# A two-block model in fp32 on one core: first block reordered, gates by tanh, linear-attention levels in 32-column tiles

## The reference, cut to what matters

```python
h = x
for i in range(DEPTH):                       # 2
    proj = rmsnorm(h, norm_g[i]) @ w_in[i]
    # hq, hf, hi: linear attention, 4 heads of 128;  hgo, hz: its gates
    # nq, kcm, vcm, ksl, vsl, kwn, vwn, ngate: sparse attention, 8 query heads of 64, 2 key heads;  nz: its gate
    log_f = log(lb + (1 - lb) * sigmoid(hf)); k = (1 - lb) * sigmoid(-hf)
    # S_t = diag(f_t) S_{t-1} + k_t v_t^T,  o_t = S_t^T q_t
    o_hg  = rmsnorm(hgrn2_chunkwise(hq, log_f, k, hi), hgrn_onorm_g[i])
    y_hg  = o_hg * sigmoid(hgo) * silu(hz)
    # o_cmp over 15 compressed blocks, o_slc and o_win over the tokens (causal)
    y_nsa = (g0 * o_cmp + g1 * o_slc + g2 * o_win) * silu(nz)
    h = h + concat([y_hg, y_nsa]) @ w_out[i]
    h = h + sigmoid(rmsnorm(h, ple_norm_g[i]) @ w_pg[i]) * (p[i] @ w_pp[i])
```

## Time and profile before

| | us |
|---|---|
| median of 3 runs | 1172.01 (1171.93 to 1172.96) |
| the profiled execution | 1172.76 |
| its span, first to last instruction | 1170.9 |
| TensorE busy | 1080.4 |
| vector engine busy | 704.9 |
| scalar engine busy | 580.2 |

### The profile page before, as it was taken

How to read it: one execution, slowest core, us unless ns; L and a number is a source line. 1 busy time by engine, 2 the same in 40 slices (tenths; PEclk the granted TensorE clock), 3 DMA queues, 4 the chain that set the end, 5 groups by cost and what they waited for, 6 DMA issues and landing times.

```text
span 1170.9 us, 20111 instructions
## 1 busy us (share of the span) xinstructions
PE 1080.4 (92%) x8425; PEld 1021.6 (87%) x8425; DVE 704.9 (60%) x1011; ACT 580.2 (50%) x818; POOL 4.9 (0%) x13
## 2 busy tenths in 40 slices
PE   3999888798998887998999999999899899999997
PEld 3998776798997776998998999999888689999996
DVE  5566555656566555567675766666544547676674
ACT  4533455555524446365744555454544536455543
POOL 1000000000000000000000000000000000000000
PEclk8999899899999999899999999999898899999998
DMA  8542522244544321263463655556244335555530
GB/s 284 170 120 71 189 72 73 72 129 147 175 115 137 99 84 61 73 211 104 133 209 126 198 182 180 185 184 193 74 149 140 108 108 165 189 185 181 179 108 36
DMA packets 144741, 163.91 MB, mean 140 GB/s; under 512 B 6072, under 2 KB 135424, under 8 KB 144672
## 3 DMA queue, kind: packets, MB, share of 16 engines
q1 hardware_dynamic: 143752, 161.46, 43.0%
q10 hardware_dynamic: 632, 1.30, 0.3%
q0 software_dynamic: 288, 0.14, 0.0%
HBM read 161.85 MB, written 1.05 MB: 139 GB/s over the span
## 4 chain that ended last, share of the span: by engine, by line
PE 74%; DVE 10%; ACT 9%; issue 3%; DMA 2%; SPq 1%; ACTq 0%; DVEq 0%
PE ps L423 22%; PE ps L424 21%; PE ps L425 21%; ACT panels_high L1093 3%; DVE panels_low L1562 3%; ACT probs L1079 2%; PE ps L626 2%; PE ps L503 2%; PE ps L439 1%; DMA panels<-in_w_in 1%; DVE neg_max L1585 1%; DVE probs L1601 1%; PE ps L509 1%; PE ps L986 1%; DVE gate_o L2038 1%
## 5 line engine op out<-in xcount | busy, mean ns | idle before, releaser
L423 PE MATMUL ps<-input_high,panels_low 128*128 128x256 f32 x1792 | 523.0, 292 | 31.1 <-DVE input_low L1542 14.2
L424 PE MATMUL ps<-input_low,panels_high 128*128 128x256 f32 x1792 | 514.8, 287 | 0.0
L425 PE MATMUL ps<-input_high,panels_high 128*128 128x256 f32 x1792 | 514.7, 287 | 0.0
L1562 DVE TENSOR_TENSOR panels_low<-panels,panels_high 128x2048 fp32r<-128x2048 f32 (+1 forms) x146 | 330.3, 2265 | 277.9 <-ACT panels_high L1093 271.2
L423 PEld LDWEIGHTS ps<-input_high,panels_low 128*128 128x128 f32 x1792 | 351.8, 196 | 38.8 <-issue 26.4
L424 PEld LDWEIGHTS ps<-input_low,panels_high 128*128 128x128 f32 x1792 | 351.8, 196 | 0.8 <-issue 0.5
L425 PEld LDWEIGHTS ps<-input_high,panels_high 128*128 128x128 f32 x1792 | 351.5, 196 | 0.0
L1093 ACT CAST panels_high<-panels 128x2048 fp32r<-128x2048 f32 (+1 forms) x146 | 274.6, 1882 | 148.4 <-PE ps L425 128.3
L423 PE MATMUL ps<-ffn_hidden_high,panels_low 128*128 128x256 f32 x352 | 100.7, 286 | 3.8 <-DVE ffn_hidden_low L2052 3.8
L424 PE MATMUL ps<-ffn_hidden_low,panels_high 128*128 128x256 f32 x352 | 101.0, 287 | 0.0
L425 PE MATMUL ps<-ffn_hidden_high,panels_high 128*128 128x256 f32 x352 | 100.8, 286 | 0.0
(11 more groups left out here) (271 smaller groups left out, 1120.3 us busy)
## 6 DMA issues: line engine op xcount, KB each, us to landing
panels<-in_ffn_up SPq DMA_DIRECT2D x44, 1024.0 KB, 5.1
panels<-in_w_in SPq DMA_DIRECT2D x32, 1024.0 KB, 5.5
panels<-in_ffn_down SPq DMA_DIRECT2D x22, 1024.0 KB, 4.9
panels<-in_mix_w_in SPq DMA_DIRECT2D x20, 1024.0 KB, 5.4
panels<-in_w_out SPq DMA_DIRECT2D x8, 1024.0 KB, 5.1
panels<-in_w_pg SPq DMA_DIRECT2D x8, 1024.0 KB, 5.2
panels<-in_mix_w_out SPq DMA_DIRECT2D x8, 1024.0 KB, 6.3
panels<-in_w_pp SPq DMA_DIRECT2D x2, 1024.0 KB, 5.0
```

Of the source, the lines that this page charges most:

```text
L423: pe.matmul(dst, w[1], x[0], start=start, stop=False if not kw else True, **kw)
L424: pe.matmul(dst, w[0], x[1], start=False, stop=False if not kw else True, **kw)
L425: return pe.matmul(dst, w[0], x[0], start=False, stop=stop, **kw)
L1562: V.tensor_tensor(low_slots[slot][:, 0:size], raw[n % SLOTS][:, 0:size], high_slots[slot][:, 0:size].bitcast(F32), ALU.subtract).then_inc( ...
```

## The change

It does six things in the first block.

- Levels by blocks of 32 tokens. Levels 0 to 5 are computed for the four diagonal 32x32 blocks alone, each in its own 32-column tile of the array, and copied under a narrower mask (32 columns a head in place of 128) into a new buffer `decay_blocks` (`AB`). Level 6 computes two 32x32 blocks, level 7 one of 64x64, and both are copied without a mask straight to `AD`. ACT spreads the blocks of `AB` into `AD` (`spread`, four copies).
- Order on TensorE. Gate chunks stand after `hid4`, after the rotated queries, after the last level, after `cross`, after the outputs, after unit 0, and in rounds 0 to 5. `hid` comes ahead of the rotation; `kc` and `vc` ahead of the last level, `kcss` right after the third chunk, `oss` after the scores of compressed keys. `hgo0` uses bank 6, `kc` and `kcss` bank 5.
- Gates by tanh. ACT copies `hz` and `nz` as they are and takes tanh(x/2) from the same bank; one more tanh covers `hgo`. DVE then uses sigmoid(x) = (1 + tanh(x/2))/2, with the factors put in the last product.
- The mixing is spread over the rounds: `mix` halves in rounds 2 and 3, `nsa_gate` halves in rounds 4 and 5, the first two quarters split after round 5.
- The first two output panels are cut by rows (`output_rows`): their first four row blocks are multiplied in round 6 and after round 7, the rest after the last unit. Banks 2 to 5.
- Norm sums of the residual use bank 0, and `pp` banks 7, 6, 1 and 2.

```diff
@@ levels on TensorE
                     for j in range(4):
                         s = (2 * g + j // 2) * T + (j % 2) * P
-                        ins = pe.matmul(ps[b][:, j * P:(j + 1) * P], KQ[:, s:s + P], QP[:, s:s + P],
-                                        start=True, stop=True)
+                        if n < NBLK_LVL:
+                            where = [(BLK * c, BLK, j * BLK, s + BLK * c, s + BLK * c) for c in range(NBLK)]
+                        elif n == NBLK_LVL:
+                            where = [(64 * e, BLK, j * BLK, s + 64 * e, s + 64 * e + BLK) for e in range(2)]
+                        else:
+                            where = [(0, 64, j * 64, s, s + 64)]
+                        for row, w, col, k, q in where:
+                            ins = pe.matmul(ps[b][row:row + w, col:col + w], KQ[:, k:k + w], QP[:, q:q + w],
+                                            start=True, stop=True, tile_position=(0, row), skip_group_check=True)
@@ gate chunks
-                    b = 1 if key[0] == "hgo0" else 0
+                    b = 6 if key[0] == "hgo0" else 0
@@ after hid4
                 todo(("hidden_parts",))
+                gate_chunk()
                 some(1)
+                (hid, as below)
                 (rotated queries)
                 some(1)
-                drained(pe, f"hid4_{l}")
-                begin(f"hid_{l}", 3)
-                ...
-                todo(("hidden",))
+                gate_chunk()
                 (rotated keys)
                 todo(("k_pad",))
-                gate_chunk()
+                pe.wait_ge(w2_landed, 48 * (l + 1))
+                pe.wait_ge(hidden_ready, l + 1)
+                product(f"kc_{l}", 5, 32, W2[:, 0:P], HID[:, 0:32])
+                product(f"vc_{l}", 3, 64, HIDV[:, :], W2[:, P:P + 64])
+                todo(("cmp_kv",))
                 some(16)
                 gate_chunk()
+                pe.wait_ge(kcsq_ready, l + 1)
+                product(f"kcss_{l}", 5, 32, head_ones, KC[:, 32:64])
+                todo(("kc_norm",))
                 (cross)
+                todo(("spread",))
                 todo(("cross",))
+                gate_chunk()
                 ...
+                pe.wait_ge(spread_ready, l + 1)
                 (outputs)
                 todo(("o_square",))
                 gate_chunk()
                 (scores of compressed keys)
-                gate_chunk()
+                pe.wait_ge(osq_ready, l + 1)
+                for g in range(2):
+                    product(f"oss{g}_{l}", 5 + g, 512, ones, SQ[:, g * 512:(g + 1) * 512])
+                todo(("o_norm",))
                 unit(0)
+                gate_chunk()
                 (transposes of the compressed probabilities)
-                gate_chunk()
@@ the rounds
+                def output_rows(g, ks):
+                    key, b = (f"wo{g}", l), out_banks[g]
+                    if ks[0] == 0:
+                        begin(f"wo_{l}_{g}", b)
+                        split(key)
+                    for j in range(2):
+                        for k in ks:
+                            pe.wait_ge(y_ready, 4 * l + k // 2 + 1)
+                            ins = product3(...)
+                    if ks[-1] == ND - 1:
+                        done(f"wo_{l}_{g}", ins)
+                        release(key)
                 for u in range(8):
                     todo(("normalise", u))
                     if u < 7:
                         unit(u + 1)
-                    else:
-                        todo(("mix",))
                     gate_chunk()
+                    if u == 0:
+                        todo(("gate_tanh",))
+                    if u in (2, 3):
+                        todo(("mix", u - 2))
+                    if u in (4, 5):
+                        todo(("nsa_gate", u - 4))
+                    if u == 6:
+                        output_rows(0, range(0, 4))
                     if u > 0:
                         weigh(u - 1)
                     turn(f"n{l}", u, pidx + u)
                     todo(("turned", u))
-                    if u == 6:
-                        todo(("sigmoids",))
+                    if u == 5:
+                        todo(("mixed",))
+                output_rows(1, range(0, 4))
                 weigh(7)
                 todo(("on",))
+                for ks in (range(4, 6), range(6, 8)):
+                    for g in range(2):
+                        output_rows(g, ks)
-                output(f"wo_{l}_", l, 2)
+                norm_sum(nidx, 0, (0,))
+                for g in (2, 3):
+                    two_chunks(f"wo_{l}_{g}", out_banks[g], (f"wo{g}", l))
+                    norm_sum(nidx, 0, (g - 1,))
@@ ACT
+                    if step == "copy" and arg[0] in tanh_dest:
+                        name = f"{arg[0]}_{l}"
+                        full(act, name)
+                        nc.scalar.copy(dest[arg[0]], bank(name)[:, :])
+                        f(tanh_dest[arg[0]], bank(name)[:, :], ACT.Tanh, scale=0.5).then_inc(free(name), 1)
+                    elif step == "spread":
+                        act.wait_ge(level_ready, 16 * l + 2 * NBLK_LVL)
+                        for c in range(NBLK):
+                            r = slice(BLK * c, BLK * (c + 1))
+                            ins = nc.scalar.copy(v3(AD, 8)[r, :, r], v3(AB, 8)[r])
+                        ins.then_inc(spread_ready, 1)
+                    elif step == "gate_tanh":
+                        f(SG[:, :], SG[:, :], ACT.Tanh, scale=0.5).then_inc(sig_ready, 1)
@@ DVE
                     elif kind == "mix":
+                        s = slice(arg[0] * 512, (arg[0] + 1) * 512)
+                        link(V.scalar_tensor_tensor(HZ[:, s], FG[:, s], 1.0, HZ[:, s], ALU.add, ALU.mult))
+                        link(V.scalar_tensor_tensor(HZ[:, s], SG[:, s], 1.0, HZ[:, s], ALU.add, ALU.mult))
+                        V.scalar_tensor_tensor(Y[:, s], QP[:, s], 0.25, HZ[:, s], ALU.mult,
+                                               ALU.mult).then_inc(yf_ready, 1)
+                    elif kind == "nsa_gate":
+                        link(V.scalar_tensor_tensor(NZ[:, s], VH[:, s], 1.0, NZ[:, s], ALU.add, ALU.mult))
+                    elif kind == "mixed":
+                        mixed_low(l, 0)
+                        mixed_low(l, 1)
                     elif kind == "on":
+                        full(dve, f"on1_{l}")
+                        V.scalar_tensor_tensor(Y[:, 1536:2048], bank(name)[:, :], 0.5, NZ[:, 512:1024],
+                                               ALU.mult, ALU.mult).then_inc(free(name), 1)
+                        mixed_low(l, 2)
                         mixed_low(l, 3)
```

More of the change, by code:

```diff
@@ L28 @@
 NLVL = 8
+BLK = 32
+NBLK = P // BLK
+NBLK_LVL = 6
 ALU = mybir.AluOpType
@@ L725, in _ @@
                 todo(("hidden_parts",))
+                gate_chunk()
                 some(1)
+                drained(pe, f"hid4_{l}")
+                begin(f"hid_{l}", 3)
+                for kv in range(2):
+                    ins = pe.matmul(ps[3][:, kv * 32:(kv + 1) * 32], HP[:, kv * P:(kv + 1) * P],
+                                    const("sum_of_four"), start=True, stop=True)
+                done(f"hid_{l}", ins)
+                todo(("hidden",))
                 pe.wait_ge(rope_ready, l + 1)
@@ L736, in _ @@
                 some(1)
-                drained(pe, f"hid4_{l}")
-                begin(f"hid_{l}", 3)
-                for kv in range(2):
-                    ins = pe.matmul(ps[3][:, kv * 32:(kv + 1) * 32], HP[:, kv * P:(kv + 1) * P],
-                                    const("sum_of_four"), start=True, stop=True)
-                done(f"hid_{l}", ins)
-                todo(("hidden",))
+                gate_chunk()
                 pe.wait_ge(k_rope_ready, l + 1)
@@ L781, in _ @@
                 todo(("o_square",))
-                pe.wait_ge(kcsq_ready, l + 1)
-                product(f"kcss_{l}", 0, 32, head_ones, KC[:, 32:64])
-                todo(("kc_norm",))
                 gate_chunk()
-                pe.wait_ge(osq_ready, l + 1)
-                for g in range(2):
-                    product(f"oss{g}_{l}", 5 + g, 512, ones, SQ[:, g * 512:(g + 1) * 512])
-                todo(("o_norm",))
                 pe.wait_ge(kc_ready, l + 1)
```

100 lines of the change are left out of this document (52 added, 48 removed).

## The result

| | before | after |
|---|---|---|
| median, us | 1171.97 (1170.58 to 1172.96, 4 runs) | 1158.22 (1155.53 to 1159.57, 4 runs) |
| ratio | | 0.9888, interval 0.9867 to 0.9909 |
| the profiled execution | 1172.76 | 1159.57 |
| its span | 1170.9 | 1157.7 |

The account below looks back on a forecast made before the run. TensorE's work (92% busy), its waits and its clock were taken to bound the kernel. Levels -5.2, walk -5.0 and clock +1.7 gave -8.5 us from the 1172.01 median: 1163.5 us, range 1152 to 1175.

Parts of the forecast that it names:

- The levels on TensorE: Narrow column tiles: 0.2 us less for each of 13 levels a layer, 5.2 less in all (10.4 less to 5.2 more).
- narrow tiles cheap, waits milder: Rival: levels 0.4 us less each, 5.2 more gained, two bank-0 waits shrink by 3 us; 1155 us, chance 0.23.
- my sum: Levels -5.2, walk -5.0, one more half-clock phase +1.7: -8.5 us, thus 1163.5 us; chance 0.46.
- The vector engine's copies: Narrower masked level copies on DVE: 6 us a layer saved, only 0.3 to 0.4 on a chain, contained in the walk.
- The walk: Reordered work from the hidden products on: waits 19.8 and clock 5.3 where 27 were, 2.5 us less a layer.
- compressed keys, for the hidden values: After two gate chunks, TensorE waits 1.9 us for DVE's low parts, level and hidden activation.
- chunk 3, bank 0 behind the last level: The third gate chunk waits 2.9 us until DVE has copied the last level out of bank 0.
- chunk 7, bank 0 behind the tanh: Chunk 7 waits 3.3 us for bank 0, behind ACT's exponentials, copies, table load and tanh; clock 1.7.
- turn 4: In round 4, cast, low part, mixing step and normalising stand in a row: TensorE waits 4.0 us, clock 1.7.
- The clock: One more half-clock phase over both layers, for waits not charged: 1.7 us more.
- The rival in which it decides: Vector queue feeds the clock: 15 half-clock phases for seven, 13.6 us more, 1177 us; decides from five more; chance 0.11.
- The tables: First tanh loads once, replacing the sigmoid's load; rival with loads at each tanh: 15 us more, 1178 us, chance 0.03.

Follow-up runs that it names:

- the mended kernel: The kernel after, with low parts behind the next unit's row maxima and hidden values ahead of casts and low parts: 1123.33 us, ratio 0.9590.
- copies padded: The kernel after with one more 128x256 VectorE product ahead of each copy of levels 0 to 5: 1157.79 us, ratio 0.9891.

## Why the prediction was right

**The levels on TensorE** were the term that was mis-sized. I had 0.2 us less for each of 13 levels a layer, with bounds of 0.4 less and 0.2 more; on the average it is 0.40. In layer 0 the first two, which stand together, give 1.2, the next 0.42, nine give 0.30 to 0.36 each, and the last, which has half the instructions and hidden products in tiles of the same width right behind it, 0.77: 5.2 us. The pace was near: eight quartets in at most 0.39 are at most 0.049 us each, for the 0.055 taken half-way down from the earlier trace rows. The entries were not. I had added 0.09 for entering, 0.09 for leaving and a few hundredths of stagger; between chunks entering takes the 0.09, and with leaving it is 0.11 in all. On the other side I took 0.89 for every level before, and most were 0.82.

Not all of this arrives. In layer 0 it is 4.13: a wait of 1.4 us for ScalarE's copy of the transposed embeddings (0.3 before) takes 1.1, since the copy comes when it came and TensorE earlier, and I did not look there. In layer 1, 3.07 arrive: 0.5 goes into the wait of a level for VectorE (1.84 for 1.35), and the mean clock there is 0.96. In the mended kernel, with the same wait and a clock of 1.00, it is 4.53. So -7.2 us for the -5.2 of the sum. That these are so near is in part luck: the tiles give some 10 us, twice the forecast, and waits and clock that I had not charged take 3.

**The rival *narrow tiles cheap, waits milder*** (1155) is nearer to the 1158.22 than my sum (1163.5), and the gain of a level is the 0.4 that it named. Its reason holds in part. A quartet takes up to 0.049 us, not the 0.03 of its moving columns, and of its 3 us for milder waits at bank 0 about 1 a layer is there (1.95 for 2.9, and 3.25 for 3.3).

By the Trainium skill's overhead, estimated from "TensorEngine Tiling (Array Packing)", Performance Considerations, a level would have been 0.8 us before the drains. The rows say 0.39, and 0.83 when neighbours share a tile: tile by tile it comes out as by that overhead, and four tiles in turn share it. Whether it is that overhead or the loading of weights that fills the 26 ns no run separates.

**The vector engine's copies** save 0.44 each (733 to 298 ns) and are off the path, as said; *copies padded* shows it.

**The walk.** The waits, in order, forecast and measured in layer 0:

| place | forecast | measured |
|---|---|---|
| compressed keys, for the hidden values | 1.9 | 3.11 |
| chunk 3, bank 0 behind the last level | 2.9 | 1.95 |
| chunk 7, bank 0 behind the tanh | 3.3 | 3.25 |
| turn 0 | 1.0 | 0.17 |
| turn 2 | 1.6 | 1.44 |
| round 4, bank 0 | 1.3 | 0.48 |
| turn 4 | 4.0 | 3.80 |
| output rows, weighing of unit 6, third quarter | 1.2, 1.2, 1.4 | 0.96, 0.88, 1.40 |
| sum | 19.8 | 17.4 |

Each named wait is there, with the named engine behind it (the first shows as "issue" in the list; VectorE writes the hidden values up to 125.3, and the product starts at 125.42). Counted from the hidden products, these values come at 17.9 us where I had 17.1, and chunk 3 starts at 22.1 for 21.2: the first two waits are off by 1 us each to opposite sides, and together by 0.3. The walk is 3.04 and 3.37 us shorter where 2.5 were forecast, and the stretch from the hidden products to the end of the second output panel (107.42 to 221.60) is 114.2 us at a mean clock of 0.91: near the 115 forecast, inside the 110 to 120 and above the 0.88 named as the edges. The named waits came out 2.4 us lower than forecast in all. The clock, which by my balance gave 1.2 us a layer (5.3 lost for 6.5; 8.2 times 83% is 6.8), gave nothing: the walks run at 0.92 both, where before had 0.94 and 0.92.

**The clock** was given one more half-clock stretch, 1.7 us. By the mean clocks of the profiled runs there are 97 us at 1.2 GHz for 91: two stretches more than before, about 3 us. But the other runs of after have 76 to 97, so that the change costs any clock is not shown. The rival in which it decides needed five stretches more and is out.

**The tables** came as forecast: ScalarE's groups from 60 to 250 us show one load at the first tanh (L1124) and two at the norms' own places (L1174), at 1283 ns each, and none between, where exponentials and tanh alternate. The Trainium skill, "ScalarE: Activation LUTs", Table sets, puts tanh and exp in one set; the trace agrees.

Of the 5.2 us between forecast and result, 2.0 are the levels, 1.4 the walks, and 1.7 what I had added apart for the clock, which the measured stretches already contain: that is all of it.

## What to carry to other kernels

These small products in column tiles paid only when neighbours went to different tiles: go round the tiles, innermost. Measure what is replaced at each of its places, too: the levels before took from 0.82 to 0.98 us, and one row stood for all. Before you judge a reordering by its waits, look at which queue holds a long, patient job (here a low part waiting for a cast) ahead of a short urgent one, and move that first; the bank freed ahead of it only moved the wait. And price a wait of TensorE together with the stretch at 1.2 GHz that follows it: in the two walks 11.8 us of waits went and 9 us of clock with them. But compare the clocks of several runs before you lay a single stretch to an edit.

## What the hardware showed

- 32 instructions of 32 columns on four 32-column tiles in turn take 0.39 us; tile by tile 0.83, as long as 8 of 128 columns (0.82). Changing to the tiled form and back costs 0.11 us between gate chunks, 0.09 of it on the way in.
- Taking away 11.8 us of TensorE's waits took 20.7 us off the two walks, where the mean granted clock rose from 0.92 to 0.96, and 23.8 us off the time.
- The clock of a stretch whose code and waits were the same was 1.00 in one kernel and 0.96 in another. Runs of one kernel differ as well: 0.958 to 0.967 over the whole, 76 to 97 us at 1.2 GHz. What starts such a fall stays open.
